# A stick-breaking attention layer on one Trainium2 core: the scores of a slot are computed one slot ahead, and GpSimd's second weight remainder of a unit moves behind an attention product

## What is computed

```python
h = rmsnorm(x, norm_g[0])
q, k, v, gate = jnp.split(h @ w_in, 4, axis=-1)          # 16 heads x 64
for every block of 128 queries:
    mask = key_pos[None, :] < q_pos[:, None]
    z = einsum('bhqd,bhkd->bhqk', qb, k) * scale
    log_beta = log_sigmoid(z)
    log_1m = where(mask, log_beta - z, 0.0)
    after = cumsum(log_1m, axis=3, reverse=True) - log_1m
    a = where(mask, exp(log_beta + after), 0.0)
    o = einsum('bhqk,bhkd->bhqd', a, v)
y = (o * silu(gate)) @ w_out
out = rmsnorm(x + y, final_g)
```

## Time and profile before

| | us |
|---|---|
| median of 3 runs | 701.91 (701.83 to 701.91) |
| the profiled execution, its own time | 702.83 |
| its span, first to last instruction | 701.0 |
| PE busy | 673.1 (96%) |
| DVE busy | 483.1 (69%) |
| ACT busy | 426.4 (61%) |
| POOL busy | 308.0 (44%) |
| mean granted PE clock | 0.992 of full speed |

### The profile page before, as it was taken

How to read it: one execution, slowest core, us unless ns; L and a number is a source line. 1 busy time by engine, 2 the same in 40 slices (tenths; PEclk the granted TensorE clock), 3 DMA queues, 4 the chain that set the end, 5 groups by cost and what they waited for, 6 DMA issues and landing times.

```text
span 701.0 us, 10872 instructions
## 1 busy us (share of the span) xinstructions
PE 673.1 (96%) x3426; PEld 565.2 (81%) x3426; DVE 483.1 (69%) x636; ACT 426.4 (61%) x795; POOL 308.0 (44%) x225
## 2 busy tenths in 40 slices
PE   5999999999999999999999999999999997999995
PEld 4787888888888888888888888888888776888884
DVE  5835657786678676867677667766776798735565
ACT  5614757676767676767676767666766674622322
POOL 2122544555464546454655464546363643315100
PEclk9999999999999999999999999999999998999998
DMA  7131310141114111510042014201421148522342
GB/s 284 46 95 41 94 43 16 63 119 32 31 57 124 31 32 37 135 39 22 23 135 60 15 31 120 75 15 30 120 60 30 60 136 295 201 91 90 121 146 95
DMA packets 28122, 57.64 MB, mean 82 GB/s; under 512 B 3376, under 2 KB 3376, under 8 KB 28080
## 3 DMA queue, kind: packets, MB, share of 16 engines
q1 hardware_dynamic: 25312, 51.13, 24.2%
q10 hardware_dynamic: 2736, 6.03, 2.3%
q0 software_dynamic: 32, 0.00, 0.0%
HBM read 37.23 MB, written 11.53 MB: 70 GB/s over the span
## 4 chain that ended last, share of the span: by engine, by line
PE 67%; DVE 12%; POOL 10%; issue 7%; ACT 3%; DMA 1%; POOLq 0%; DVEq 0%; ACTq 0%
PE proj_ps L486 31%; PE t_ps L644 8%; PE o_ps L632 8%; PE z_ps L561 8%; DVE rest L1016 7%; PE z_ps L581 5%; POOL a_group L1115 5%; POOL w_split L1091 5%; PE proj_ps L561 4%; PE o_ps L486 2%; DVE aT L1000 1%; DMA a_group<-x 1%; ACT stage L719 1%; ACT gate L776 1%; DVE gate L982 1%
## 5 line engine op out<-in xcount | busy, mean ns | idle before, releaser
L486 PE MATMUL proj_ps<-hT,w_split 128*128 128x512 f32 x1464 | 359.9, 394 | 2.1 <-DVE hT L889 1.4
L486 PEld LDWEIGHTS proj_ps<-hT,w_split 128*128 128x128 f32 x1464 | 269.9, 188 | 57.6 <-DVE hT L889 2.3
L1115 POOL TENSOR_TENSOR a_group<-a_group,rest 128x128 f32<-128x128 f32 (+7 forms) x128 | 160.6, 1257 | 279.2 <-DVE rest L1016 279.2
L1016 DVE TENSOR_TENSOR_SCAN rest<-rest,restart 128x128 f32<-128x128 f32 (+7 forms) x128 | 213.4, 1668 | 16.0 <-ACT rest L809 15.5
L1091 POOL TENSOR_TENSOR w_split<-w_raw,w_split 128x512 fp32r<-128x512 f32 x64 | 115.6, 1807 | 38.0 <-DVE w_split L851 38.0
L1000 DVE TENSOR_TENSOR aT<-t_ps,aT 128x512 fp32r<-128x512 f32 (+2 forms) x160 | 93.2, 607 | 40.1 <-ACT aT L794 38.8
L794 ACT ACTIVATE aT<-t_ps 128x512 fp32r<-128x512 f32 (+2 forms) x160 | 80.2, 532 | 65.8 <-PE t_ps L644 64.6
L581 PE MATMUL z_ps<-arena 128*128 128x512 f32 (+2 forms) x384 | 96.3, 366 | 0.3 <-DVE arena L938 0.3
L938 DVE TENSOR_TENSOR arena<-stage,arena 64x512 fp32r<-64x512 f32 x64 | 43.9, 686 | 69.4 <-ACT arena L739 68.8
L644 PE MATMUL t_ps<-ident,a_group 128*128 128x128 f32 x576 | 84.9, 275 | 4.7 <-POOL a_group L1115 4.4
L809 ACT ACTIVATE rest<-z_ps 128x128 f32<-128x128 f32 (+7 forms) x128 | 83.9, 655 | 8.9 <-PE z_ps L581 8.6
(11 more groups left out here) (86 smaller groups left out, 454.2 us busy)
## 6 DMA issues: line engine op xcount, KB each, us to landing
w_raw<-w_in SPq DMA_DIRECT2D x64, 256.0 KB, 2.7
arena<-arena SPq DMA_DIRECT2D x32, 256.0 KB, 4.3
wo_raw<-w_out SPq DMA_DIRECT2D x16, 256.0 KB, 3.7
o_hi_scratch<-o_split SPq DMA_DIRECT2D x14, 256.0 KB, 2.1
o_lo_scratch<-o_split SPq DMA_DIRECT2D x14, 256.0 KB, 2.4
hT<-o_hi_scratch SPq DMA_DIRECT2D x14, 256.0 KB, 4.9
hT<-o_lo_scratch SPq DMA_DIRECT2D x14, 256.0 KB, 5.8
a_group<-x SPq DMA_DIRECT2D x14, 256.0 KB, 3.4
```

Of the source, the lines that this page charges most:

```text
L486: mm = nc.tensor.matmul(bank[:, :], w_split[:, ring, wl, b, :], hT[:, hl, b, half * HALF:(half + 1) * HALF], start=(b == 0 and n == 0), st ...
L1016: nc.vector.tensor_tensor_scan(span, span, restart[:, S - 1:(S - 1 - width if width < S else None):-1], 0.0, ALU.mult, ALU.max).then_inc(s ...
L1115: nc.gpsimd.tensor_tensor(a, a, rest[:, s % 2, S + 1 - width:S + 1], ALU.mult).then_inc(a_ready, 1)
```

## The change

On PE, slot s now computes z(s+1) behind its projection and ahead of its attention outputs, where z(s) had stood ahead of the projection. Slot 15 computes z(0) of the next pair. The double call in slots 0 and 8 goes. In slot 0 of pair 0 the order stays projection, z(0), z(1).

On POOL, lo_w part 0 stays behind a(s) of slots 1, 5, 9, 13; part 1 moves from behind a(s) of slots 2, 6, 10, 14 to behind a(s) of slots 3, 7, 11, 15. ACT still makes the hi part in slots 2, 6, 10, 14. Nothing is added or left out.

```diff
             def slot(p, par, s):
-                q_late = is_first(p) and s == 0
-                if q_late:
-                    project_part(p, s)
-                if not is_tail(p):
-
-                    for block in {0: (s, s + 1), 1: ()}.get(s % 8, (s,)):
-                        scores(p, par, block)
                 if v_t_at(p, s) is not None:
                     t = v_t_at(p, s)
 
                     transpose_v(t_base(p) + t, t % 2, 2 * UNITS0 + 8 * p + 2 + (s == 8), int(s == 8))
-                if not is_tail(p) and s in proj_slots(p) and not q_late:
+                if not is_tail(p) and s in proj_slots(p):
                     project_part(p, s)
                 if isinstance(p, int):
                     for _ in range(EARLY_BY_SLOT.get((p, s), 0)):
                         project_out(*early.pop(0))
+
+                if is_first(p) and s == 0:
+                    scores(p, par, s)
+                if s < SLOTS - 1 and not is_tail(p):
+                    scores(p, par, s + 1)
+                elif not is_last(p) and not is_tail(p):
+                    scores(p + 1, 1 - par, 0)
 
                 for t, av, ahh, grp, j in av_at(p, s):
...
-                if s % 4 in (1, 2) and not is_last(p):
-                    n = 2 * (UNITS0 + 4 * p + s // 4 + 1) + s % 4 - 1
-                    lo_w(n, (UNITS0 + 1 + s // 4) % 2, s % 4 - 1)
+                if s % 2 and not is_last(p):
+                    part = s % 4 // 2
+                    lo_w(2 * (UNITS0 + 4 * p + s // 4 + 1) + part, (UNITS0 + 1 + s // 4) % 2, part)
```

## The result

| | us |
|---|---|
| before, median of 8 runs | 701.91 |
| changed, median of 8 runs | 704.21 (most between 703.46 and 704.52) |
| ratio, 95% interval | 1.0028 (1.0017 to 1.0039) |
| forecast | 713.0 (703.5 to 717.5) |

The change makes the kernel 0.3% slower. The sign was forecast; the size was about five times too large. One of the 8 runs, the profiled one, took 760.62 us at a mean granted PE clock of 0.847, so the profile after is that of a second measurement of the same kernel (label changed_again, 704.01, ratio 1.0025, 1.0016 to 1.0034). That execution itself took 703.45 us, span 701.4.

A forecast was written before the change was run, and what follows sets the result against it. PE was taken as the bound, with what it waits for. Terms 5.4 + 3.3 + 0.3 + 0.1 + 1.1 + 1.5 = 11.7 us on 701.91 gave 713.6, rounded down to 713.0, range 703.5 to 717.5.

The forecast's parts named there:

- Transposes and outputs later: T(s) ends later on PE by the scores ahead of it; ACT's sigmoid of slot 15 starts 0.45 us later.
- Slots 13 to 17, +0.9 a pair: DVE and POOL's serial chain makes lo_w part 1 late for P(17): +0.9 us in pairs 1 to 6, 5.4 us.
- Slots 5 to 9, +0.55 a pair: The same chain makes lo_w late for P(9), at 235.3 against 234.75: +0.55 us in six pairs, 3.3 us.
- the sum's order: At slots 7 to 9: a(7), scan of 128, lo_w; at 15 to 17: gate product, a(15), scan of 128, lo_w.
- The projections keep their places: On PE, T(s) ends later by the scores while the projections stay where they were; no time charged for it.
- each link's early end: Rival "The chains don't pile up": scan(14) and scan(15) go at their early bounds; about +2.4 us, 704.3; chance 0.23.
- Evacuation: P(16) waits for the copy of `stage` and stays put; z(17)'s 0.3 us no longer fills that gap, comes behind it.
- Into the last pair: Its P(1) needs only part 0; a(15) of pair 6 ends 0.15 later: +0.1 us, between -0.6 and +0.2.
- The last pair's long wait: PE's 4.2 us wait for DVE grows by z(5)'s 0.77 and the same exclusions: +1.1 us, between 0 and +1.8.
- The end: Slots 12, 14 and the tail's T(0) each take the sigmoid's shift of 0.45 to 0.55: +1.5 us, +0.5 to +2.
- The rival "Faster": The exclusion lifts, lo_w part 1 comes ahead of P(9) and P(17), PE wins the 4.4 us: 699.6; chance 0.05.
- The page's rule: DVE and GpSimd exclude each other for whole instructions; by it the sum would be some 2.5 us higher.

The follow-up runs named there:

- the scores at the slot's end: The changed kernel with z(s+1) moved behind the transposes T(s), at the slot's end, so nothing of attention is late; 700.37 us, ratio 0.9975.
- the remainder alone: The kernel before with only GpSimd's second remainder moved, behind a(3), a(7), a(11), a(15); scores as before; 697.99 us, ratio 0.9939.
- the last pair in the old order: The changed kernel with pair 7 computing its scores as before, z(s) ahead of its slot's projection and two in slot 8; 702.66 us, ratio 1.0006.
- the scores alone: The changed kernel with GpSimd's second remainder back in slots 2, 6, 10, 14, so only the scores are one slot ahead; 710.70 us, ratio 1.0118.
- the order of the prediction: The changed kernel with all three orders the prediction's sum took for slots 7 to 9 and 15 to 17 forced by waits; 712.64 us, ratio 1.0152.
- the scan ahead of the remainder: The changed kernel with lo_w part 1 of slots 7 and 15 made to wait for DVE's scan of 128; 707.27 us, ratio 1.0065.

## Why the prediction was wrong

- **Transposes and outputs later: right.** The copy of T(14)'s block started 0.36 us behind P(15)'s first matmul (262.42 against 262.06), where it had stood 0.66 ahead of it, and the sigmoid 0.64 behind it, against 0.20: 0.44 later, forecast 0.45. It is a real cost: 3.6 us come back when the transposes are early again (700.37 against 704.01).
- **Slots 13 to 17, +0.9 a pair: right in kind, 0.37 in size.** Scan(14), a(14) and scan(15) ended 0.3 to 0.4 us sooner than forecast (266.36 against 266.7 for the last). The failed step is the chain behind them: "a(15) takes 2.0, till 269.35. The scan of 128, waiting since 267.6, takes 0.3. Only then comes lo_w part 1, 1.29 us, till 270.9. PE has it at 271.05". At four of the six places this is the order that ran, and P(17) still came 8.37 us behind P(15), not 8.91. The 0.54 us are four steps: the gate product ended 0.10 sooner, a(15) took 1.86 behind it and not 2.0, scan and remainder together 1.35 and not 1.55, and PE started 0.05 behind the remainder and not 0.15. The second came from a misread row: of a(15) in the earlier trace rows 1.86 us lie behind the gate product's end (267.32 to 269.18), not 2.0. The third was in the rows that the prediction quotes: a remainder issued early ended 1.08 us after the scan, but the sum charged it 1.29.
- **Slots 5 to 9, +0.55 a pair: wrong, nothing came.** Its chain has the same full durations ("lo_w at 235.15", 1.3 us behind the scan). The order was another one too: the scan of 128 was issued 0.04 us ahead of a(7). But by pair 0, where the sum's order ran, that is worth 0.13 us of the 0.57; 0.29 are the remainder's full time behind the scan. P(9) stood at 234.84, and did not wait.
- **"The projections keep their places": a term put at nothing.** The slots between (9 to 15 and 1 to 7) became 0.33 us a pair shorter, and why is open.
- Over six pairs, in the sum's terms: +8.7 forecast; 3.2 less at P(17), 3.4 less at P(9), 2.0 less in the slots between; 0.2 measured. I had priced each link's early end (704.3) and given it 0.23. Its number came true by luck: scan(14) and scan(15) did not go at their early bounds (2.65 and 2.60 us, blocked), P(17) was 0.37 late and not 0.2, and the shorter slots between are not in it.
- **Evacuation: right in kind.** P(16) and slot 8's transposes of v wait for `stage`; 0.3 us each, shown with the scores at the slot's end.
- **Into the last pair: +0.1 forecast, -0.3 measured** (35.40 to 35.11).
- **The last pair's long wait: +1.1 forecast, +0.45 measured.** The wait itself stayed 4.2. DVE's chain behind it came 0.37 us later and no exclusion was added: in slot 5 the scan of 768 was issued 0.06 us ahead of the output gating (570.75 and 570.81), as before (570.38 and 570.43), and each instruction behind it takes what it took before.
- **The end: +1.5 forecast, +0.8 measured**, at the places forecast (0.76 at slot 12, 0.31 at slot 14, 0.54 in the tail). The last pair's order as a whole is worth 1.35 us (702.66 against 704.01).
- **The rival "Faster"** had the remainder leave the scans' time free and nothing else late. That is what the remainder's move does alone: 697.99.
- **The page's rule.** The Trainium skill, SBUF — State Buffer, section "Who interferes with whom", calls the port that the two engines share an exclusive lock, which the loser waits out. The prediction says that its sum goes by the row and would be 2.5 us higher by the page. It is not so: the sum charges the remainder its full 1.29 us, as the page would. The rows agree on the exclusion (the remainder's 3.32 us of the earlier trace rows, where 1.29 is its time alone) and are a little milder on its length, see below.

## What to carry to other kernels

Where two engines exclude each other, charge the blocked instruction what a row shows past the end of the one ahead of it, not its whole time: a chain of four such steps was 0.5 us too long here. Moving an operand ahead does nothing for a consumer whose own program order still puts another input first; look at what the moved work pushes back and what it no longer covers (here the transposes and the evacuation gap, +8.4 us together). Measure two edits of one change apart before judging it: here -4.3 and +8.4 hid behind +1.7. And an order forced by an added wait has the price of the wait in it: look for a place where the order was the same already, and subtract what it costs there.

## What the runs showed of the hardware

- A GpSimd remainder that was issued while a DVE instruction held it off ended less than its own time (1.27 to 1.29 us) after that instruction's end: 1.07 us after the scan of 128, 1.13 after a gate product, 1.08 after the long scan of the earlier trace rows. Held back by a semaphore instead, it ended 1.43 us after the scan: 0.16 us until its start, then 1.27. Why the early one is shorter is not shown.
- After the same wait of 4.2 us in the last pair PE's granted clock came back at different times. In rows of 1 us it stands at 0.50, the lower of its two levels (1.2 GHz of 2.4), from 585 to 591 before, and from 586 to 588 in the change (0.58 from 588 to 589); PE started again at 585.26 and 585.63. Stretch, length, busy time of each engine, granted clock, DMA share, GB/s; before, then changed:

```profile
588.00:592.00 4.00, 4.00 (x15) 3.20 (x14) 3.19 (x5) 1.98 (x5) 0.93 (x1) 0.62 0.96 313
```

```profile
588.00:592.00 4.00, 4.00 (x22) 3.42 (x22) 3.56 (x5) 2.54 (x6) 0.94 (x1) 0.90 0.94 318
```

The two T groups behind the wait are 5.60 us apart before (585.86 to 591.46) and 4.77 after. Of the other profiles with PE's old order there, 4.8 stands in the remainder alone and in the last pair in the old order. Of those with the order of the change, 4.7 stands in the scores alone and in the order of the prediction, and 6.11 in the scan ahead of the remainder. So 0.8 to 1.4 us of one execution are decided there, enough for the two profiled executions to lie on either side of their medians (702.83 to 701.91; 703.45 to 704.01). What decides it stays open; it was not tried.
